# Recurrence gates of a hybrid attention and recurrence block: two passes per head over 64 rows in place of two over 128

## The chip, the cores and the metric

The kernel runs on one core of a Trainium2 chip. TensorE (PE) multiplies, VectorE (DVE), ScalarE (ACT) and GpSimd (POOL) do the rest, SyncE (SP), ScalarE and GpSimd issue transfers. The metric is the time of one execution on the device in microseconds.

## The reference

One layer: RMS norm, a combined projection, 16 heads of forgetting attention beside a recurrence over 1024 channels, an output projection, and a gated MLP with a convolution. All is float32, 512 tokens. The change is in the two gates of the recurrence:

```
def rg_lru(x, w_a, b_a, w_x, b_x, lam):
    xb = xf.reshape(B, S, N_RNN_BLOCKS, RNN_BLOCK)            # 16 blocks of 64 channels
    r = sigmoid(einsum('bsni,nij->bsnj', xb, w_a).reshape(B, S, D_RNN) + b_a)
    i_g = sigmoid(einsum('bsni,nij->bsnj', xb, w_x).reshape(B, S, D_RNN) + b_x)
    log_a = -RG_C * r * softplus(-lam)
    a = exp(log_a)
    mult = sqrt(-expm1(2.0 * log_a))
    bterm = mult * i_g * xf
    ...
```

So each block of 64 channels has a 64x64 matrix for each of two gates.

## The kernel before

Everything is computed transposed, with channels on the partitions and 512 tokens along the free axis. A float32 product is made of three TensorE passes: each operand is split into a rounded high part (ScalarE, `hi`) and the rest (VectorE, `lo`), and `product` adds high by high, high by low and low by high.

The mixer (the first 560 us) goes over 8 pairs of heads. A pair has 128 attention channels and 128 recurrence channels, and ten units of weights (512 KB each): two for each of x, q, k, v and the branch that goes through GeLU. SyncE loads a unit into `raw`, ScalarE's `split` writes the high part into `w_all`, VectorE's `split` the low part, and TensorE's `unit` waits for `split_done` and makes 48 passes of 256 columns. `w_all` holds two units, so ScalarE may write the next one only when `unit_used` says that TensorE is through with the one before last. Pair 0 is written out in the opening, pair 1 is `pair(1, True)`, and pairs 2 to 7 are a hardware loop over `pair(p, False)`. Each engine has its own `pair`, written by hand, and its own order.

For pair p, u is 10 p. TensorE makes units u and u+1 (x), transposes of the probabilities of the pair before, u+2 and u+3 (q), the attention values of the pair before, u+4 with the gates in its middle and u+5 (k), then u+6 with the scores in its middle and u+7 (v), transposes, u+8 and u+9. In pair 1 the gates stand in the middle of u+5.

The gates: `gw` holds for each gate a 128x128 matrix with the two 64x64 blocks of the pair on its diagonal and zeros beside them. It is loaded by GpSimd, split by ScalarE (`gate_weights`, `gw_hi`) and VectorE (`gw_lo`). TensorE's `gates` multiplies it with the convolved x (`xc_hi`, `xc_lo`), one bank for each gate. ScalarE's `gates` turns the banks into `rg` and `ig` by a sigmoid with a bias for each channel, lines 801 and 802. In the loop ScalarE's next piece of work behind them is the split of unit u+6; in pair 1 it is `k_hi`. GpSimd issues the load of `gw` for pair p, then that of `negc`, and then three rounds of sums of weights in memory, each of which waits for transfers. In the opening the load of `gw` is GpSimd's first instruction, and the memset of `ones` comes behind it; TensorE's `keep_busy` (18 float32 products of `ones`, before any work) waits for that memset.

The scores of a pair (line 2152) already run with 64 rows for each of two heads, the two heads' passes one after another into different banks.

Of the kernel before, what the change touches and what calls it, by code (L numbers as in the profile page):

```python
# [24 lines left out]
F32R = mybir.dt.float32r  # L25
ALU = mybir.AluOpType
ACT = mybir.ActivationFunctionType
AXX = mybir.AxisListType.X

P = 128  # L30
# [5 lines left out]
HD = 64  # L36
# [132 lines left out]
def block_kernel(nc, xT, par_d, weights, gate_w, out):  # L169
# [5 lines left out]
    with ExitStack() as ctx:  # L175
        def sb_in(stack, name, shape, dt=F32):
            return stack.enter_context(nc.sbuf_tensor(name, [P, *shape], dt))
# [38 lines left out]
        mix = ExitStack()  # L216
# [4 lines left out]
        xc_hi = sb_in(mix, "xc_hi", [S], F32R)  # L221
        xc_lo = sb_in(mix, "xc_lo", [S], F32R)
        gel = sb_in(mix, "gel", [S])
        rg = sb_in(mix, "rg", [S])
        ig = sb_in(mix, "ig", [S])
# [14 lines left out]
        sm = sb_in(mix, "sm", [CAUSAL])  # L240
        negc = sb_in(mix, "negc_sb", [2, S])
        pick = sb_in(mix, "pick", [2, P])
        gw = sb_in(mix, "gw", [2, P])
        gw_hi = sb_in(mix, "gw_hi", [2, P], F32R)
        gw_lo = sb_in(mix, "gw_lo", [2, P], F32R)
        stats = sb_in(mix, "stats", [3, QT])
        lam4 = sb_in(mix, "lam4", [NP])
        lam8 = sb_in(mix, "lam8", [NP])
# [9 lines left out]
        start = ExitStack()  # L258
# [102 lines left out]
        def col(name, i=0):  # L361

            c = COLS[name] + i
            return par[:, c:c + 1] if isinstance(c, int) else par[:, bass.ds(c, 1)]
# [222 lines left out]

        @block.gpsimd
        def _(pool):
            pool.dma_start(gw[:], gate_w[0]).then_inc(gw_landed, 16)  # L590
            pool.memset(eps[:], EPS)
            pool.memset(ones[:], 1.0).then_inc(consts_set, 1)
            pool.memset(ident[:], 0.0).then_inc(zeros_set, 1)
# [41 lines left out]
            sums(0, 2)  # L635
            for p in range(1, NP):
                pool.wait_ge(gw_split, p)
                pool.dma_start(gw[:], gate_w[p]).then_inc(gw_landed, 16)
                pool.wait_ge(s_taken, p * 6)
                pool.dma_start(negc[:], negc_d[2 * p:2 * p + 2].partition_broadcast(P)).then_inc(negc_landed, 16)  # L640
                sums(3 * p - 1, 3 * p + 2)
# [124 lines left out]
        def _(act):  # L766
# [30 lines left out]

            def gates(p, a, b):

                act.wait_ge(gates_done, p)  # L800
                act.activation(rg[:], a[:], ACT.Sigmoid, bias=col("b_a", p - 1)).then_inc(gates_taken, 1)
                act.activation(ig[:], b[:], ACT.Sigmoid, bias=col("b_x", p - 1)).then_inc(gates_taken, 1)

            def gate_exponentials(p):

                act.wait_ge(gates_taken, p * 2)
                act.activation(tt[:], rg[:], ACT.Tanh, scale=one_col(lam4, p - 1)).then_inc(gate_funcs, 1)
                act.activation(ae[:], rg[:], ACT.Exp, scale=one_col(lam8, p - 1)).then_inc(gate_funcs, 1)

# [6 lines left out]
                act.activation(gel[:], ev[:], ACT.Gelu_apprx_tanh).then_inc(gel_done, 1)  # L816

            def gate_weights(p):
                act.wait_ge(gw_landed, p * 16 + 16)
                act.activation(gw_hi[:], gw[:], ACT.Copy).then_inc(gw_hi_done, 1)  # L820

            def high_of(dst, src, taken, p, done):
# [340 lines left out]
            for i in range(NF):  # L1163
# [21 lines left out]
                if NS <= i < NS + 2 * PAIRS_OUT:  # L1185
                    n = i - NS
# [882 lines left out]
        def _(pe):  # L2069
            def product(dst, a, b, start, stop, goes_on=False):  # L2070

                (ah, al), (bh, bl) = a, b
                pe.matmul(dst, ah, bh, start=start, stop=False, skip_group_check=goes_on)  # L2073
                pe.matmul(dst, ah, bl, start=False, stop=False, skip_group_check=goes_on)  # L2074
                return pe.matmul(dst, al, bh, start=False, stop=stop, skip_group_check=goes_on)  # L2075
# [110 lines left out]
            def gates(p, a, b):  # L2186
                pe.wait_ge(gw_split, p + 1)
                pe.wait_ge(xc_split, p + 1)
                for g, bank in enumerate((a, b)):
                    last = product(bank[:], (gw_hi[:, g], gw_lo[:, g]), (xc_hi[:], xc_lo[:]), True, True)  # L2190
                last.then_inc(gates_done, 1)

            def pair_gates(p):
                pe.wait_ge(pt_split, p * 6)
# [2 lines left out]
            def pair_scores(p):  # L2197
                pe.wait_ge(q_split, p + 1)
                pe.wait_ge(k_split, p + 1)
                pe.wait_ge(gates_taken, p * 2 + 2)  # L2200
                scores((0, 1))

            def pair(p, first):
# [89 lines left out]
            gates(0, PT[0], PT[2])  # L2293
            unit(7, 1, 1, SB[2], False, True, middle=forget_back)
            pe.wait_ge(negc_ready, 1)
            pe.wait_ge(gates_taken, 2)
            for e, bank in enumerate((PT[0], PT[2])):
                last = pe.matmul(bank[:], pick[0:2 * NP, e], tt[0:2 * NP], start=True, stop=True)
            last.then_inc(negc_spread, 1)
# [30 lines left out]
            for c in range(3):  # L2330
                pe.wait_ge(split_done, N_OUT + c + 1)
                for j in range(4):
                    last = out_opening(c, j)
# [12 lines left out]
            for k in range(UK):  # L2346
                last = by_tokens(PJ[0], w_tile(0, k), k, k == 0, k == UK - 1)
            last.then_inc(unit_used, 1)
            pe.wait_ge(split_done, N_OUT + 6)
            for k in range(UK, KT):  # L2350
# [4 lines left out]
                last = by_tokens(PT[0], (w3_hi[:, i // 2, i % 2], w3_lo[:, i // 2, i % 2]), k, k == UK, k == KT - 1)  # L2355
# [17 lines left out]
            for n, bank in enumerate((OUT_BANKS[3][1], LAST_BANK)):  # L2373
                c = slice(HS * n, HS * n + HS)
                for i in range(UK):
                    last = product(bank[:, c], w_tile(1, i), (act_hi[:, UK + i, c], act_lo[:, UK + i, c]), i == 0,
                                   i == UK - 1)
# [6 lines left out]
            for j in range(QT):  # L2384
                if j == 0:
                    pe.wait_ge(osq_done, KT)
                if j == QT // 2:
                    pe.wait_ge(osq_done, KT + 1)
                last = pe.matmul(SB[2][:, j:j + 1], sq[:, 0, P * j:P * j + P], ones[:, 0:1], start=False, stop=j == QT - 1,
                                 skip_group_check=True)  # L2390
# [7 lines left out]
            for m in range(OPEN):  # L2398
                pe.wait_ge(split_done, N_FF + m + 1)
                for kt in range(2):  # L2400
                    k = 2 * m + kt
                    if k == 0:
# [4 lines left out]
                        for i, bank in enumerate((SB[0], SB[1], PT[0], PT[1])):  # L2407
                            last = half_by_tokens(bank, w_tile(0, 2 * i), 0, 1, True, False)
                        continue
                    pe.wait_ge(act_split, AFTER_Y + k + 1)  # L2410
                    for i, bank in enumerate((SB[0], SB[1], PT[0], PT[1])):
                        last = by_tokens(bank, w_tile(m % 2, 2 * i + kt), k, False, k == KT - 1)
# [160 lines left out]
```

## Time and profile before

| | us |
|---|---|
| median of 3 runs (lowest, highest) | 2149.89 (2149.03, 2150.46) |
| the profiled execution, its own time | 2149.89 |
| its span, first to last instruction | 2148.1 |
| TensorE busy in the span | 2116.0 |
| VectorE busy | 1685.9 |
| ScalarE busy | 1017.9 |
| GpSimd busy | 346.8 |

The granted clock of TensorE is 0.993 of full speed over the span. Times in the rows are counted from the span's start. A row of a timeline gives the start, the duration, the engine, the line and operation, output and inputs, the tile shape (rows by columns), the count where several are merged, and in brackets the idle time of that engine before it with what ended it. The duration of a TensorE pass includes its fill and drain, and passes overlap: what a pass costs is the distance to the next one's start, about 0.11 us for 256 columns and 0.23 us for 512.

### The profile page before, as it was taken

The page shows a single profiled execution, that of the slowest core. Times are in us where ns is not written, and L with a number is a line of the kernel's source. Part 1 is how long each engine was busy: PE and PEld are TensorE (multiplying, and loading weights), DVE is VectorE, ACT ScalarE, POOL GpSimd, SP SyncE. Part 2 cuts the span into 40 slices and gives each one's busy share as a digit, 9 for nine tenths or more (in the row PEclk, how much of TensorE's full clock was granted, in tenths as well). Part 3 has the DMA queues.
Part 4 walks back from the last instruction along what each step waited for, and adds up shares of the span by engine and source line. Part 5 has one row for each costly group of instructions (what it writes and reads, how often), then busy time and mean ns, then how long its engine had stood idle before and what let it go on. Part 6 is the DMA issues. An engine that isn't in the chain of part 4 may idle for free.

```text
span 2148.1 us, 44222 instructions
## 1 busy us (share of the span) xinstructions
PE 2116.0 (99%) x18226; PEld 2091.2 (97%) x18226; DVE 1685.9 (78%) x2298; ACT 1017.9 (47%) x1281; POOL 346.8 (16%) x431
## 2 busy tenths in 40 slices
PE   9999999999999999999999999999999999999995
PEld 8999999999999999999999999999999999999995
DVE  7777777778855877888888888888887767768886
ACT  6555554456322554444444444444444545445442
POOL 0222222222100001111111111211212001112003
PEclk9999999999999999999999999999999999999997
DMA  5788989888543436888878888787888658679544
GB/s 178 171 187 208 207 188 207 196 188 188 162 123 98 156 108 184 221 224 214 218 218 216 222 225 214 219 216 215 247 211 272 190 167 277 179 190 300 177 142 169
DMA packets 238755, 423.84 MB, mean 197 GB/s; under 512 B 17009, under 2 KB 151793, under 8 KB 237313
## 3 DMA queue, kind: packets, MB, share of 16 engines
q0 software_dynamic: 88224, 159.97, 35.9%
q1 hardware_dynamic: 147776, 256.84, 35.8%
q10 hardware_dynamic: 2592, 4.72, 0.6%
q8 instruction: 120, 1.97, 0.4%
q14 instruction: 43, 0.34, 0.1%
HBM read 382.64 MB, written 89.16 MB: 220 GB/s over the span
## 4 chain that ended last, share of the span: by engine, by line
PE 93%; DVE 3%; issue 1%; ACT 1%; POOL 1%; DMA 1%; POOLq 0%; DVEq 0%; ACTq 0%
PE bank L2073 29%; PE bank L2075 29%; PE bank L2074 29%; PE bank L2457 2%; PE bank L2152 1%; PE bank L2165 1%; DVE w_all L1219 1%; DMA act_lo_f<-t_spill 1%; PE bank L2177 0%; PE bank L2176 0%; ACT act_hi L1140 0%; ACT w_all L771 0%; PE bank L2237 0%; POOL act_lo_f L762 0%; POOL tsum_f L762 0%
## 5 line engine op out<-in xcount | busy, mean ns | idle before, releaser
L2073 PE MATMUL bank<-act_hi,w_all 128*128 128x256 f32 x3272 | 910.1, 278 | 4.8 <-DVE w_all L1219 2.2
L2074 PE MATMUL bank<-act_lo,w_all 128*128 128x256 f32 x3272 | 903.8, 276 | 0.0
L2075 PE MATMUL bank<-act_hi,w_all 128*128 128x256 f32 x3272 | 903.8, 276 | 0.0
L2073 PEld LDWEIGHTS bank<-act_hi,w_all 128*128 128x128 f32 x3272 | 614.3, 188 | 11.2 <-issue 3.7
L2074 PEld LDWEIGHTS bank<-act_lo,w_all 128*128 128x128 f32 x3272 | 614.4, 188 | 0.7 <-issue 0.2
L2075 PEld LDWEIGHTS bank<-act_hi,w_all 128*128 128x128 f32 x3272 | 614.4, 188 | 0.0
L2073 PE MATMUL bank<-tsum,w_all 128*128 128x256 f32 x1280 | 353.5, 276 | 0.0
L2075 PE MATMUL bank<-tsum,w_all 128*128 128x256 f32 x1280 | 353.3, 276 | 0.0
L2074 PE MATMUL bank<-tsum,w_all 128*128 128x256 f32 x1280 | 353.3, 276 | 0.0
L1134 ACT ACTIVATE w_all<-raw_s 128x1024 fp32r<-128x1024 f32 x172 | 182.7, 1062 | 243.3 <-PE bank L2075 222.7
L1219 DVE TENSOR_TENSOR w_all<-raw,w_all 128x1024 fp32r<-128x1024 f32 x134 | 164.0, 1224 | 133.6 <-ACT w_all L771 131.6
L1862 DVE TENSOR_TENSOR w_all<-raw_s,w_all 128x1024 fp32r<-128x1024 f32 x172 | 210.4, 1224 | 68.9 <-ACT w_all L1134 67.6
L2074 PEld LDWEIGHTS bank<-tsum,w_all 128*128 128x128 f32 x1280 | 240.2, 188 | 0.0
L2073 PEld LDWEIGHTS bank<-tsum,w_all 128*128 128x128 f32 x1280 | 240.2, 188 | 0.0
L2075 PEld LDWEIGHTS bank<-tsum,w_all 128*128 128x128 f32 x1280 | 240.2, 188 | 0.0
L771 ACT ACTIVATE w_all<-raw 128x1024 fp32r<-128x1024 f32 x133 | 140.6, 1057 | 162.4 <-PE bank L2075 157.5
L2073 PE MATMUL bank<-tsum,w 128*128 128x256 f32 x656 | 181.7, 277 | 0.2 <-DVE pu L1935 0.2
L2075 PE MATMUL bank<-tsum,w 128*128 128x256 f32 x656 | 181.2, 276 | 0.0
L2074 PE MATMUL bank<-tsum,w 128*128 128x256 f32 x656 | 181.2, 276 | 0.0
L2073 PE MATMUL bank<-act_hi,w 128*128 128x256 f32 x568 | 157.3, 277 | 0.0
L2075 PE MATMUL bank<-act_hi,w 128*128 128x256 f32 x568 | 156.8, 276 | 0.0
L2074 PE MATMUL bank<-act_lo,w 128*128 128x256 f32 x568 | 156.8, 276 | 0.0
(390 smaller groups left out, 3513.0 us busy)
## 6 DMA issues: line engine op xcount, KB each, us to landing
raw<-weights SPq DMA_DIRECT2D x262, 512.0 KB, 4.4
w_sums<-weights POOLq DMA_DIRECT2D x96, 512.0 KB, 7.0
raw_s<-weights SPq DMA_DIRECT2D x84, 512.0 KB, 5.7
raw_s<-weights POOLq DMA_DIRECT2D x84, 512.0 KB, 5.8
raw_a<-weights SPq DMA_DIRECT2D x66, 512.0 KB, 5.7
raw_s<-w_sums SPq DMA_DIRECT2D x48, 512.0 KB, 5.0
t_spill<-h_out POOLq DMA_DIRECT2D x48, 256.0 KB, 3.7
act_lo_f<-t_spill POOLq DMA_DIRECT2D x11, 1024.0 KB, 9.1
```

The costliest lines, as they stand in the source:

```text
L771: act.activation(w_hi[s], k_tiles(raw[:, s]), ACT.Copy).then_inc(hi_done, 1)
L1134: act.activation(w_slot(q)[0], k_tiles(RAW_OF[n](i)), ACT.Copy).then_inc(hi_done, 1)
L1219: dve.tensor_tensor(w_lo[s], k_tiles(raw[:, s]), word(w_hi[s]), ALU.subtract).then_inc(split_done, 1)
L1862: dve.tensor_tensor(lo, k_tiles(RAW_OF[n](i)), word(hi), ALU.subtract).then_inc(split_done, 1)
L2073: pe.matmul(dst, ah, bh, start=start, stop=False, skip_group_check=goes_on)
L2074: pe.matmul(dst, ah, bl, start=False, stop=False, skip_group_check=goes_on)
L2075: return pe.matmul(dst, al, bh, start=False, stop=stop, skip_group_check=goes_on)
L2152: last[e] = pe.matmul(dst, q, k, start=t == 0, stop=t == 2)
L2165: last = pe.transpose(dst, sm[:, c:c + P], ident[:])
L2457: last = pe.matmul(region, w[:, k // 2, k % 2], summed[:, k], start=start and k == 0, stop=k == UK - 1, skip_group_check=not start)
```

## The change

The two blocks of a gate no longer stand in one 128x128 matrix. For the even head `gw` holds on partitions 0 to 63 both gates' blocks side by side (64x128), for the odd head on partitions 64 to 127 the same with the gates exchanged. One pass over 64 rows gives both gates of one head. The products of the even head go to bank a (r gate on rows 0 to 63, i gate on rows 64 to 127), those of the odd head to bank b (i gate on rows 0 to 63, r gate on 64 to 127), the three parts of the product outermost, the two heads alternating. ScalarE now has four sigmoids of 64 rows, GpSimd three loads in place of one, and `gw`, `gw_hi` and `gw_lo` have 128 columns in place of 256.

```
-            pool.dma_start(gw[:], gate_w[0]).then_inc(gw_landed, 16)
+            def load_gates(p):
+                pool.dma_start(gw[0:HD], gate_w[p, 0:HD, :, 0:HD]).then_inc(gw_landed, 16)
+                for g in range(2):
+                    pool.dma_start(gw[HD:P, 1 - g], gate_w[p, HD:P, g, HD:P]).then_inc(gw_landed, 16)
+            load_gates(0)
...
-                act.wait_ge(gates_done, p)
-                act.activation(rg[:], a[:], ACT.Sigmoid, bias=col("b_a", p - 1)).then_inc(gates_taken, 1)
-                act.activation(ig[:], b[:], ACT.Sigmoid, bias=col("b_x", p - 1)).then_inc(gates_taken, 1)
+                act.wait_ge(gates_done, p * 2)
+                h0, h1 = slice(0, HD), slice(HD, P)
+                for dst, bias, parts in ((rg, "b_a", ((h0, a, h0), (h1, b, h1))), (ig, "b_x", ((h0, a, h1), (h1, b, h0)))):
+                    for h, bank, at in parts:
+                        act.activation(dst[h], bank[at], ACT.Sigmoid, bias=col(bias, p - 1)[h]).then_inc(gates_taken, 1)
...
-                for g, bank in enumerate((a, b)):
-                    last = product(bank[:], (gw_hi[:, g], gw_lo[:, g]), (xc_hi[:], xc_lo[:]), True, True)
-                last.then_inc(gates_done, 1)
+                for t, (w, x) in enumerate(((gw_hi, xc_hi), (gw_hi, xc_lo), (gw_lo, xc_hi))):
+                    for e, bank in enumerate((a, b)):
+                        h = slice(HD * e, HD * e + HD)
+                        last = pe.matmul(bank[:], w[h].rearrange("p a n -> p (a n)"), x[h], start=t == 0, stop=t == 2)
+                        if t == 2:
+                            last.then_inc(gates_done, 1)
```

The waits on `gw_landed`, `gates_done` and `gates_taken` have the new counts; nothing else moves. Line numbers of the changed kernel are a little higher.

TensorE in the loop, in the middle of unit u+4, before. Banks 5 and 6 are a and b, bank 3 takes k:

```order
L2075 MATMUL bank3<-act_hi,w_all 128x256
L2073 MATMUL bank5<-xc_hi,gw_hi 128x512 [waits xc_split,gw_split,pt_split]
L2074 MATMUL bank5<-xc_lo,gw_hi 128x512
L2075 MATMUL bank5<-xc_hi,gw_lo 128x512
L2073 MATMUL bank6<-xc_hi,gw_hi 128x512
L2074 MATMUL bank6<-xc_lo,gw_hi 128x512
L2075 MATMUL bank6<-xc_hi,gw_lo 128x512
L2073 MATMUL bank3<-act_hi,w_all 128x256
```

The same place in the changed kernel; each row of line 2201 is a pass over 64 rows (the shape is that of the output):

```order
L2084 MATMUL bank3<-act_hi,w_all 128x256
L2201 MATMUL bank5<-xc_hi,gw_hi 128x512 [waits xc_split,gw_split,pt_split]
L2201 MATMUL bank6<-xc_hi,gw_hi 128x512
L2201 MATMUL bank5<-xc_lo,gw_hi 128x512
L2201 MATMUL bank6<-xc_lo,gw_hi 128x512
L2201 MATMUL bank5<-xc_hi,gw_lo 128x512
L2201 MATMUL bank6<-xc_hi,gw_lo 128x512
L2082 MATMUL bank3<-act_hi,w_all 128x256
```

The number of passes is the same, the banks alternate. ScalarE in the loop, from the squares to the split of unit u+6 (the row of `w_all`), before:

```order
L842 ACTIVATE sq<-y_t 128x512
L801 ISA [waits gates_done]
L801 ACT_TABLE_LOAD
L801 ACTIVATE rg<-bank5,par 128x512
L802 ISA
L802 ACTIVATE ig<-bank6,par 128x512
L769 ISA
L145 REGISTER_ALU [waits raw_landed0]
L771 ACTIVATE w_all<-raw 128x4x2x128 [waits unit_used]
```

And in the changed kernel:

```order
L851 ACTIVATE sq<-y_t 128x512
L807 REGISTER_ALU
L811 ISA [waits gates_done]
L811 ACT_TABLE_LOAD
L811 ACTIVATE rg<-bank5,par 64x512
L811 ISA
L811 ACTIVATE rg<-bank6,par 64x512
L811 ISA
L811 ACTIVATE ig<-bank5,par 64x512
L811 ISA
L811 ACTIVATE ig<-bank6,par 64x512
L776 ISA
```

Two sigmoids and three register instructions more stand ahead of that split. GpSimd at the start of the program, before:

```order
L588 UNCONDITIONAL_BRANCH
L590 DMA gw<-gate_w 128x256
L591 MEMSET eps 128x1
L592 MEMSET ones 128x128
L593 MEMSET ident 128x128
```

And in the changed kernel:

```order
L589 UNCONDITIONAL_BRANCH
L593 DMA gw<-gate_w 64x2x64
L595 DMA gw<-gate_w 64x64 x2
L598 MEMSET eps 128x1
L599 MEMSET ones 128x128
```

The memset of `ones` has three issues ahead of it in place of one.

## Rows read from the trace of the kernel before

**Rows 1.** The page: busy time by engine, and the chain that ended last.
```profile
PE 2116.0 (99%) x18226; PEld 2091.2 (97%) x18226; DVE 1685.9 (78%) x2298; ACT 1017.9 (47%) x1281; POOL 346.8 (16%) x431
...
PE 93%; DVE 3%; issue 1%; ACT 1%; POOL 1%; DMA 1%; POOLq 0%; DVEq 0%; ACTq 0%
```

**Rows 2.** Timeline of TensorE, pair 7: first pass of the gates, first behind them.
```profile
491.23 0.39 PE L2073 MATMUL bank<-xc_hi,gw_hi 128*128 128x512 f32 x1
...
492.63 0.28 PE L2073 MATMUL bank<-act_hi,w_all 128*128 128x256 f32 x1
```

**Rows 3.** Timeline of TensorE, pair 7: into the scores and out of them.
```profile
503.48 0.28 PE L2075 MATMUL bank<-act_hi,w_all 128*128 128x256 f32 x1
503.68 0.50 PE L2152 MATMUL bank<-k_hi,q_hi 64*128 64x512 f32 x2
...
504.49 0.34 PE L2152 MATMUL bank<-k_hi,q_hi 64*128 64x384 f32 x2
...
505.60 0.28 PE L2152 MATMUL bank<-k_hi,q_lo 64*128 64x256 f32 x2
...
506.03 0.28 PE L2074 MATMUL bank<-act_lo,w_all 128*128 128x256 f32 x1
```

**Rows 4.** Timeline of ScalarE, pair 7: attention copies, sigmoids, split of unit 76.
```profile
492.45 1.08 ACT L834 ACTIVATE sm<-bank 64x512 f32<-64x512 f32 x2
...
497.19 0.69 ACT L801 ACTIVATE rg<-bank,par 128x512 f32<-128x512 f32 x1
497.78 0.68 ACT L802 ACTIVATE ig<-bank,par 128x512 f32<-128x512 f32 x1
498.35 1.06 ACT L771 ACTIVATE w_all<-raw 128x1024 fp32r<-128x1024 f32 x1
```

**Rows 5.** Timelines of VectorE and TensorE: unit u+6 in pairs 7 and 2.
```profile
499.44 1.23 DVE L1219 TENSOR_TENSOR w_all<-raw,w_all 128x1024 fp32r<-128x1024 f32 x1 [2.63 <-ACT w_all L771]
...
500.83 0.28 PE L2073 MATMUL bank<-act_hi,w_all 128*128 128x256 f32 x1
...
181.89 1.23 DVE L1219 TENSOR_TENSOR w_all<-raw,w_all 128x1024 fp32r<-128x1024 f32 x1 [2.63 <-ACT w_all L771]
...
183.17 0.38 PE L2073 MATMUL bank<-act_hi,w_all 128*128 128x256 f32 x1
183.39 0.28 PE L2074 MATMUL bank<-act_lo,w_all 128*128 128x256 f32 x1
```

**Rows 6.** Timelines of ScalarE and VectorE, pair 7: the split of unit 72.
```profile
468.69 1.06 ACT L771 ACTIVATE w_all<-raw 128x1024 fp32r<-128x1024 f32 x1 [0.46 <-PE bank L2075]
...
469.79 1.23 DVE L1219 TENSOR_TENSOR w_all<-raw,w_all 128x1024 fp32r<-128x1024 f32 x1 [2.20 <-ACT w_all L771]
```

**Rows 7.** Timelines of GpSimd, VectorE and TensorE: the start, and a small load.
```profile
1.27 0.68 POOL L590 DMA_DIRECT2D gw<-gate_w  x1 [0.81 <-POOLq L2565]
...
63.32 0.53 POOL L614 DMA_DIRECT2D negc<-tt  x1 [20.78 <-DVE tt L1300]
...
7.40 0.68 DVE L1507 TENSOR_TENSOR w_all<-raw,w_all 128x512 fp32r<-128x512 f32 x1
...
2.25 6.63 PE L2237 MATMUL bank<-ones 128*128 128x128 f32 x36 [2.25 <-POOL ones L592]
8.63 0.36 PE L2073 MATMUL bank<-act_hi,w_all 128*128 128x256 f32 x1
```

**Rows 8.** Timelines of ScalarE, VectorE and TensorE, pair 1: keys and scores.
```profile
120.65 0.63 ACT L824 ACTIVATE k_hi<-ev 128x512 fp32r<-128x512 f32 x1
...
121.31 0.69 DVE L1412 TENSOR_TENSOR k_lo<-ev,k_hi 128x512 fp32r<-128x512 f32 x1 [0.75 <-ACT k_hi L824]
...
122.43 0.50 PE L2152 MATMUL bank<-k_hi,q_hi 64*128 64x512 f32 x2
```

**Rows 9.** Timeline of ScalarE: k_hi in pair 0, split behind gw_hi in pair 1.
```profile
61.94 0.63 ACT L824 ACTIVATE k_hi<-ev 128x512 fp32r<-128x512 f32 x1 [1.51 <-DVE ev L1421]
...
106.30 1.06 ACT L771 ACTIVATE w_all<-raw 128x1024 fp32r<-128x1024 f32 x1 [1.80 <-DMA raw<-weights]
```

More of the change, by code:

```diff
@@ L242, in block_kernel @@
         pick = sb_in(mix, "pick", [2, P])
-        gw = sb_in(mix, "gw", [2, P])
-        gw_hi = sb_in(mix, "gw_hi", [2, P], F32R)
-        gw_lo = sb_in(mix, "gw_lo", [2, P], F32R)
+        gw = sb_in(mix, "gw", [2, HD])
+        gw_hi = sb_in(mix, "gw_hi", [2, HD], F32R)
+        gw_lo = sb_in(mix, "gw_lo", [2, HD], F32R)
+        sb_in(mix, "rest_of_gw", [6 * HD])
         stats = sb_in(mix, "stats", [3, QT])
@@ L637, in _ @@
                 pool.wait_ge(gw_split, p)
-                pool.dma_start(gw[:], gate_w[p]).then_inc(gw_landed, 16)
+                load_gates(p)
                 pool.wait_ge(s_taken, p * 6)
@@ L798, in gates @@
             def gates(p, a, b):
-                act.wait_ge(gates_done, p)
-                act.activation(rg[:], a[:], ACT.Sigmoid, bias=col("b_a", p - 1)).then_inc(gates_taken, 1)
-                act.activation(ig[:], b[:], ACT.Sigmoid, bias=col("b_x", p - 1)).then_inc(gates_taken, 1)
+                act.wait_ge(gates_done, p * 2)
[3 more added lines that the diff above has]
+                        act.activation(dst[h], bank[at], ACT.Sigmoid, bias=col(bias, p - 1)[h]).then_inc(gates_taken, 1)
             def gate_exponentials(p):
-                act.wait_ge(gates_taken, p * 2)
+                act.wait_ge(gates_taken, p * 4)
                 act.activation(tt[:], rg[:], ACT.Tanh, scale=one_col(lam4, p - 1)).then_inc(gate_funcs, 1)
@@ L818, in gate_weights @@
             def gate_weights(p):
-                act.wait_ge(gw_landed, p * 16 + 16)
+                act.wait_ge(gw_landed, p * 48 + 48)
                 act.activation(gw_hi[:], gw[:], ACT.Copy).then_inc(gw_hi_done, 1)
@@ L2199, in pair_scores @@
                 pe.wait_ge(k_split, p + 1)
-                pe.wait_ge(gates_taken, p * 2 + 2)
+                pe.wait_ge(gates_taken, p * 4 + 4)
                 scores((0, 1))
@@ L2295, in _ @@
             pe.wait_ge(negc_ready, 1)
-            pe.wait_ge(gates_taken, 2)
+            pe.wait_ge(gates_taken, 4)
             for e, bank in enumerate((PT[0], PT[2])):
```

## The prediction, made before the changed kernel was run

> **What bounds the kernel now.** First the page. TensorE is busy for 99% of the span and carries 93% of the chain that ended last [rows 1]. An edit pays only if it shortens TensorE's queue, and costs as soon as TensorE waits at a place where it does not wait now. ScalarE at 47% and VectorE at 78% look roomy, but those are averages. So I read next, around the gates, who releases TensorE's next weights and how long before it wants them. A unit here is one 512 KB block of weights, 48 passes of 256 columns.
>
> Take pair 7, the last turn of the loop. After the gates ScalarE converts the weights of unit 76 (the pair's u+6), VectorE subtracts, and TensorE may begin that unit. VectorE's subtraction starts at 499.44 and takes 1.23 us, so it ends at 500.67; TensorE starts the unit at 500.83 [rows 5]. The margin is 0.16 us. In pair 2 there is none: the subtraction ends at 183.12, TensorE starts at 183.17, and its next pass comes 0.22 us later where 0.11 is usual [rows 5]. Pair 4 reads as pair 2, pairs 3, 5 and 6 as pair 7. Six times the second path arrives in the very moment in which TensorE needs it.
>
> How is that path made? It starts from TensorE itself: ScalarE waits at 468.69 for the pair's first unit to be used up, and VectorE's subtraction follows at 469.79 [rows 6]. From there VectorE never idles for more than 0.2 us until 488.6, and from then on the two hand each other work (convolution, q, the two attention halves, the squares) with no wait for TensorE; ScalarE comes to its sigmoids at 497.19 straight from the squares and a table load [rows 4]. The gate products were ready at 492.6 plus the drain of the last pass, over 4 us earlier [rows 2]. So the sigmoids wait for ScalarE, not for TensorE, and everything added to them moves the end of the path.
>
> **TensorE's part of the change.** Six passes of 128 rows start at 491.23, and the next unit goes on at 492.63: 1.40 us [rows 2]. The new passes have the form of the scores: 64 rows, 512 columns, two side by side in two banks. There the last pass before starts at 503.48, so its successor would start at 503.59; three doubled steps of 512 columns are over at 504.49, which is 0.90 us with the entry [rows 3]. Leaving: the last doubled step starts at 505.60 with 256 columns, and the second pass after it at 506.03, where 505.60 + 0.12 + 0.11 = 505.83 would be natural, so 0.20 us [rows 3]. The new gates take 1.10 us, and TensorE is 0.30 us shorter each time. A doubled step alone costs half of two passes; the entry and the exit eat 0.4 of the 0.7 us.
>
> **ScalarE's part.** Two sigmoids of 128 rows become four of 64 rows. Starts are 0.59 and 0.57 us apart [rows 4]. Does half the rows halve it? The attention copies are 64x512, and two of them take 1.08 us [rows 4], so a narrow one is no cheaper than about 0.5 us. I take 2 x 0.585 = 1.17 us more; the lower bound is 4 x 0.49 - 1.17 = 0.8 (two copies, less the last one's tail), the upper 1.4 with about 0.05 us for each added register instruction, if they show.
>
> **Pairs 2 to 7.** The subtraction ends 1.17 us later: in pair 7 at 501.84, TensorE starts about 0.05 us after it as in pair 2, at 501.89, and pays the 0.11 us of a restart, against 500.83: +1.17. In pair 2, which restarts already, +1.17. TensorE arrives 0.30 us sooner, and only waits longer. The keys come next on ScalarE: k_lo ends about 1.2 us later too, and the scores then start half a unit (2.7 us) after the late start, so they don't wait a second time. After the scores TensorE makes one and a half units before it needs probabilities, and ScalarE and VectorE wait for it again; the delay isn't made up, for the next pair's path starts from TensorE. 6 x 1.17 = **+7.0 us**.
>
> **Pair 1** has another order: its unit 16 is converted before the gates, but the keys after. k_hi starts at 120.65 right behind the sigmoids, k_lo at 121.31 for 0.69 us, and the scores at 122.43 [rows 8]. 1.17 later, k_lo ends at 123.17 and the scores start at 123.2: +0.8, of which gw_lo, now half as wide and ahead of it on VectorE, gives back a little. **+0.7 us**. TensorE's 0.30 goes into that wait.
>
> **Pair 0** lies in the opening. ScalarE idles 1.51 us before k_hi [rows 9], which covers the 1.17. Should that cover go, k_hi would be late by what is missing, and the scores of the opening have several us in hand. TensorE keeps its gain: **-0.3 us**.
>
> **The loads.** One GpSimd load becomes three. At the start they stand ahead of the memset of ones that releases TensorE's warming passes. Those run from 2.25 until the first real pass at 8.63, although its weights were split at 7.40 + 0.68 = 8.08 [rows 7]. So the start hangs on GpSimd's queue. One issue takes 0.68 us there, a small one later 0.53 [rows 7]; two more cost 1.06 to 1.36, I take 1.2. The inputs have 0.55 us in hand already and now 1.7. TensorE has hardly a wait in the 70 us behind it, so nothing absorbs it: **+1.2 us**. In the loop the three loads, and the negc load and the sums queued behind them on GpSimd, come 1.1 to 1.4 us later. In pair 1 ScalarE waits for gw, but behind it 1.80 us more for raw [rows 9], which hides that; in later pairs gw_hi is followed by over 4 us of waiting for xc. If this cover were gone, pair 1 alone could lose 1 us. gw_hi and gw_lo are half as wide and lie in the same gaps in pairs 2 to 7: nothing.
>
> **Sum.** 7.0 + 0.7 + 1.2 - 0.3 = +8.6 us on the profiled execution, which took 2149.89 us (span 2148.1) and is itself the median of the three runs: **2158.5 us**, 0.40% slower. With the bounds: ScalarE at +0.8 gives 4.8 + 0.35 + 1.1 - 0.3 = +6.0; at +1.4 it gives 8.4 + 1.0 + 1.4 - 0.3 = +10.5. So 2155.5 to 2160.5.
>
> **Rivals.** (a) *The path has slack that I don't see*: VectorE makes up for the sigmoids, or the conversion of unit u+6 turns out not to end last. Then TensorE's 0.30 counts in all eight places and only the start costs: -2.4 + 1.2 = -1.2, 2148.7 us. For it: both engines have idle time on average. Against it: the rows of pair 2, where TensorE already waits.
>
> (b) *Faster*: as (a), and the doubled passes switch for nothing. One gate block then costs 3 x 0.23 = 0.70 in place of 1.40, eight save 5.6, less 1.2 at the start: -4.4, 2145.5 us. It decides as soon as ScalarE's 1.17 us is covered in the loop and the entry costs nothing. The scores, which show an entry and an exit of 0.2 us each [rows 3], speak against it.
>
> The Trainium skill, TensorE: Matmul & The Clock Gate, section Measured speedup vs the span model, has packed passes cost one pass and about 4 ns for each further tile, which is (b). TensorEngine Tiling (Array Packing), section Key Properties, says that changing the tiling mode drains the array; by that the block keeps the 1.10 us of my sum, and here the trace agrees: 0.4 us lie around each block of scores.
>
> (c) *Part of it*: half-row sigmoids run nearly in the time of the wide ones together, ScalarE adds 0.4 us or less. Pairs 2 to 7 then lose about 0.4 each, and the sum is 2.4 + 0 + 1.2 - 0.3 = +3.3, 2153.2 us. For it only that fewer rows are read; against it the copies [rows 4].
>
> (d) *The gate passes do not run side by side*, six one after another with the entry and the exit: 1.8 us where I take 1.1. In pairs 1 to 7 TensorE waits for the other path anyway, in pair 0 it costs 0.7 more: 2159.2.
>
> **Chances.** Forecast with (d) 78%, (c) 8%, (a) 9%, (b) 5%. This kernel's measurement tells some 0.2% (4.3 us) from no change, so slower by more 79%, within it 16%, faster by more 5%. The range 2153 to 2161.5 takes in (c) and the bounds with some run to run spread, and leaves (a) and (b) out.
>
> **What would show it.** In the profile after: four sigmoid rows about 0.58 us apart, and VectorE's subtraction for unit u+6 starting near 3.8 us (now 2.63) after its last work; TensorE with a wait of about 1.2 us released by that subtraction in each of pairs 2 to 7, and of about 1 us before the scores of pair 1; gate blocks of 1.1 us; the first real pass near 9.8 us instead of 8.63; a loop turn of 64.7 us where it is 63.5. Sigmoids at 0.3 us, or no wait of TensorE for the subtraction, would make the prediction wrong; so would a start that stays at 8.6.

## The result, and the profile after

| | before | after |
|---|---|---|
| median of 6 runs each (lowest, highest), us | 2150.18 (2148.33, 2150.95) | 2162.56 (2160.90, 2164.03) |
| span of the profiled execution, us | 2148.1 | 2159.0 |
| ScalarE busy, us | 1017.9 | 1029.2 |

The change costs 12.4 us, a ratio of 1.0059 with an interval of 1.0047 to 1.0070. Slower as forecast, but 4 us more than forecast, and outside the range. The profiled execution of the changed kernel took 2160.90 us, the fastest of its six, so that its trace shows 11 of the 12.4 us. One execution of the kernel before, of 27 in a later series, took 5546 us and one of eleven of e9 5407, and neither is in a ratio.

The page of the changed kernel, busy time, chain and the first row of the costliest groups (the line, then count, busy us and mean ns, then the idle time before it and who ended most of it):

```profile
PE 2113.1 (98%) x18226; PEld 2085.9 (97%) x18226; DVE 1685.7 (78%) x2298; ACT 1029.2 (48%) x1297; POOL 355.8 (16%) x447
...
PE 83%; DVE 9%; ACT 4%; issue 3%; POOL 1%; DMA 1%; DVEq 0%; ACTq 0%; POOLq 0%; SPq 0%
...
L2082 PE MATMUL bank<-act_hi,w_all 128*128 128x256 f32 x3272 | 911.2, 278 | 15.8 <-DVE w_all L1228 12.2
```

The chain, which was TensorE's at 93% [rows 1], now runs through VectorE and ScalarE for 13%. Who makes TensorE wait between 80 and 570 us, the loop of pairs, stands in the waits (us in total, times, longest):

```profile
PE bank L2082 <- DVE w_all L1228: 10.2, 6, 1.7
PE bank L2161 <- DVE k_lo L1421: 1.8, 1, 1.8
PE bank L2174 <- DVE sm L1348: 0.8, 1, 0.8
```

Six waits for the weights of unit u+6, one in each of pairs 2 to 7, and one for the keys in pair 1: the places that the prediction named. Its sizes do not fit. The third, at 95 us, for the probabilities of pair 0, is in the kernel before too, and is its only one in this stretch:

```profile
PE bank L2165 <- DVE sm L1339: 0.6, 1, 0.6
```

Pair 7, TensorE around the gates, which answers [rows 2]:

```profile
501.20 0.28 PE L2084 MATMUL bank<-act_hi,w_all 128*128 128x256 f32 x1
501.41 0.50 PE L2201 MATMUL bank<-xc_hi,gw_hi 64*128 64x512 f32 x2
501.75 0.40 PE L2201 MATMUL bank<-xc_lo,gw_hi 64*128 64x512 f32 x2
501.98 0.40 PE L2201 MATMUL bank<-xc_hi,gw_lo 64*128 64x512 f32 x2
502.31 0.38 PE L2082 MATMUL bank<-act_hi,w_all 128*128 128x256 f32 x1
502.53 0.28 PE L2083 MATMUL bank<-act_lo,w_all 128*128 128x256 f32 x1
```

The pass after the gates would follow the last one at 501.31; the second pass behind them starts at 502.53 where 502.31 + 0.11 would be natural. From 501.31 to 502.42 is 1.11 us for what took 1.40. TensorE's part is as forecast. Then ScalarE in the same pair, which answers [rows 4]:

```profile
505.98 1.28 ACT L811 ACT_TABLE_LOAD   x1
507.27 1.40 ACT L811 ACTIVATE rg<-bank,par 64x512 f32<-64x512 f32 x2
508.69 1.39 ACT L811 ACTIVATE ig<-bank,par 64x512 f32<-64x512 f32 x2
510.11 1.06 ACT L778 ACTIVATE w_all<-raw 128x1024 fp32r<-128x1024 f32 x1
```

From the first sigmoid to the split of u+6 it is 510.11 - 507.27 = 2.84 us. Before it was 1.16: 1.68 more, where the prediction has 1.17. VectorE and TensorE follow, answering [rows 5]:

```profile
511.20 1.22 DVE L1228 TENSOR_TENSOR w_all<-raw,w_all 128x1024 fp32r<-128x1024 f32 x1 [4.31 <-ACT w_all L778]
```

```profile
512.48 0.39 PE L2082 MATMUL bank<-act_hi,w_all 128*128 128x256 f32 x1 [1.70 <-DVE w_all L1228]
```

VectorE idles 4.31 us where it idled 2.63: the whole 1.68. TensorE stands still for 1.70. Pair 2 reads 186.63 with 1.72, pair 6 447.31 with 1.70. From pair 6 to pair 7 the chain needs 512.48 - 447.31 = 65.17 us, where a turn took 63.5.

Where the 11 us come from can be read off one event that both traces have, the first pass of each pair's scores (before; after; how much later):

| pair | before | after | later | added |
|---|---|---|---|---|
| 0 | 68.80 | 69.00 | 0.20 | 0.20 (0.50 by the start, 0.30 gained by the gates) |
| 1 | 122.43 | 124.42 | 1.99 | 1.79 (0.21 by the longer wait at 95 us, 1.58 behind it) |
| 2 | 186.12 | 189.59 | 3.47 | 1.48 |
| 3 | 249.62 | 254.76 | 5.14 | 1.67 |
| 4 | 313.20 | 319.92 | 6.72 | 1.58 |
| 5 | 376.73 | 385.09 | 8.36 | 1.64 |
| 6 | 440.18 | 450.26 | 10.08 | 1.72 |
| 7 | 503.68 | 515.42 | 11.74 | 1.66 |

Behind the loop the difference shrinks to 10.9. From 710.3 to 713.7 us TensorE's granted clock in before is at 1.2 GHz, which this execution of after has not, and across that stretch the difference falls from 11.74 to 11.24; the rest goes later, in small steps.

### The profile page after: what moved, and what is told of

The parts are those of the page before. It is cut to its first block, busy times and chain, and to the rows that moved or that the text cites. A ratio compares the mean times of both kernels' runs of the same rounds, so it can differ in the third digit from the quotient of the medians.

```text
span 2159.0 us, 44272 instructions
## 1 busy us (share of the span) xinstructions
PE 2113.1 (98%) x18226; PEld 2085.9 (97%) x18226; DVE 1685.7 (78%) x2298; ACT 1029.2 (48%) x1297; POOL 355.8 (16%) x447
## 4 chain that ended last, share of the span: by engine, by line
PE 83%; DVE 9%; ACT 4%; issue 3%; POOL 1%; DMA 1%; DVEq 0%; ACTq 0%; POOLq 0%; SPq 0%
PE bank L2082 26%; PE bank L2084 26%; PE bank L2083 26%; PE bank L2469 2%; DVE w_all L1228 1%; ACT w_all L778 1%; PE bank L2161 1%; DVE xc L1414 1%; DVE pt_lo L1315 0%; ACT ig L811 0%; ACT L811 0%; PE bank L2174 0%; DVE w L1381 0%; DVE y_t L1396 0%; DMA raw<-weights 0%
```

## Experiments

Every ratio is to the kernel before, measured in alternation on the same chip.

**Is it ScalarE alone, and what makes a narrow sigmoid so long?** The sigmoids of the changed kernel stand 0.71 us apart, those of before 0.58, and a narrow one takes 0.685 us, a wide one 0.69. Three kernels ask for the reason. Two change only the order of the four:

```
# as changed: (out rows, in rows) = (0,0) (64,64) (0,64) (64,0)
+ e1_out_rows: (0,0) (0,64) (64,64) (64,0)
+ e2_in_rows:  (0,0) (64,0) (64,64) (0,64)
```

> The changed kernel with ScalarE's four sigmoids in another order: r even, i even, r odd, i odd, so that the first two and the last two write the same rows, while the rows read change from each to the next. In the changed kernel the four start 0.71 us apart, the whole duration of one; before, two sigmoids of 128 rows started 0.59 us apart. Theory A (ScalarE lets the next instruction in early only if it writes the same rows): two of the four distances fall to 0.59 us, the block from 2.84 to 2.6 us, 8 us x 0.24 in all, so about 1.7 us less than the changed kernel, 2160.9. Theory B (the rows read decide): all four stay 0.71 us, and the time stays at 2162.6. Theory C (a narrow sigmoid with a bias never overlaps, in whatever order): the same as B.

> The changed kernel with the four sigmoids in the order r even, i odd, r odd, i even: the first two and the last two read the same rows of their banks, while the rows written change from each to the next. Theory A (rows written decide): all four distances stay 0.71 us, 2162.6. Theory B (rows read decide): two of them fall to 0.59 us, 2160.9. Theory C (never): 2162.6.

The third takes the kernel before and cuts each of its two sigmoids into two halves; TensorE and the loads stay.

```
-act.activation(rg[:], a[:], ACT.Sigmoid, bias=col("b_a", p - 1)).then_inc(gates_taken, 1)
-act.activation(ig[:], b[:], ACT.Sigmoid, bias=col("b_x", p - 1)).then_inc(gates_taken, 1)
+for dst, bias, bank in ((rg, "b_a", a), (ig, "b_x", b)):
+    for h in (slice(0, HD), slice(HD, P)):
+        act.activation(dst[h], bank[h], ACT.Sigmoid, bias=col(bias, p - 1)[h]).then_inc(gates_taken, 1)
```

> The kernel before with only ScalarE's part of the change: each of its two sigmoids in two halves of 64 rows, with the loads and TensorE's passes of before. If the longer sigmoid block is what costs (1.68 us more on the path to unit u+6), pairs 2 to 7 lose 1.5 to 1.6 us each, pair 1 about 1.7, pair 0 little: 2150.2 + 11 = 2161 us, nearly the whole loss. If the loads or the 64-row passes were behind a good part of it, it stays under 2157.

Measured: e1 2163.48, 1.0068 [1.0051, 1.0084]; e2 2160.98, 1.0053 [1.0036, 1.0069]; e3 2160.85, 1.0053 [1.0036, 1.0070]. So ScalarE's part alone, with no new pass on TensorE, is some 11 of the 12 us. The waits of e3, as above:

```profile
PE bank L2074 <- DVE w_all L1220: 8.5, 6, 1.4
PE bank L2153 <- DVE k_lo L1413: 1.3, 1, 1.3
```

The six are 0.3 us shorter each than in the changed kernel, because TensorE arrives later by just that. In e1 and e2 no order brings two sigmoids closer than 0.70, so A and B fall. C is left, and beside it a rule by which a change of either side is enough, since each step in both kernels changes at least one; the probe below tells the two apart. That e2's time is the one that theory B gave is luck, as its two steps did not shrink. Only one step shrinks, in e2 the last one, to the split:

```profile
507.93 0.69 ACT L810 ACTIVATE rg<-bank,par 64x512 f32<-64x512 f32 x1
508.65 0.69 ACT L810 ACTIVATE ig<-bank,par 64x512 f32<-64x512 f32 x1
509.24 1.05 ACT L778 ACTIVATE w_all<-raw 128x1024 fp32r<-128x1024 f32 x1
```

0.59 us, where all others have 0.71. That sigmoid writes from row 0 on, like the split.

**The start.** The changed kernel, with the first loads of `gw` behind the memset of ones on GpSimd:

```
-            load_gates(0)
             pool.memset(eps[:], EPS)
             pool.memset(ones[:], 1.0).then_inc(consts_set, 1)
+            load_gates(0)
```

> The changed kernel with the first three gate loads behind the memset of ones in place of ahead of it. In the changed kernel the first real pass of TensorE starts at 9.13 us, before at 8.63. The warming passes now start below 2 us and the first real pass should start at 8.1 to 8.6 us: 0.5 to 1 us less than the changed kernel, 2161.8 us. If the start is held by something else it stays at 9.1 and 2162.6.

Measured: 2162.02, 1.0057 [1.0040, 1.0073]. The first real pass starts at 8.36, in the changed kernel at 9.13 (9.55 and 9.52 in e1 and e2), before at 8.63. The scores of pair 0 start 0.67 us sooner than in the changed kernel and those of pair 1, at 123.25, 1.17 us sooner, so the start is on the path. The times do not show it (1.0057 beside the 1.0059 of the changed kernel). At the end none of it is left in the profile, and in pair 3 one sees why (a window, TensorE busy and its passes, the granted clock, the DMA engines' share, GB/s):

```profile
248.00:252.00 4.00, 1.99 (x15) 0.92 1.44 178
252.00:256.00 4.00, 4.00 (x24) 0.65 0.81 190
```

24 passes in 4 us where some 35 are usual: 3.4 us at 1.2 GHz, right behind a wait of 2.01 us that ends at 250.97. It cost this execution some 1.7 us. The other waits in the pairs, of 1.3 to 1.8 us, in this run and the others, had no such thing behind them.

**TensorE's part alone.** The changed kernel with its loads and its passes, and two sigmoids of 128 rows on the two banks. It leaves out sorting the halves of the banks into the two gates, so that only the r gate of the even head is right and the output is wrong; the work is the same:

```
-for dst, bias, parts in ((rg, "b_a", ((h0, a, h0), (h1, b, h1))), (ig, "b_x", ((h0, a, h1), (h1, b, h0)))):
-    for h, bank, at in parts:
-        act.activation(dst[h], bank[at], ACT.Sigmoid, bias=col(bias, p - 1)[h]).then_inc(gates_taken, 1)
+act.activation(rg[:], a[:], ACT.Sigmoid, bias=col("b_a", p - 1)).then_inc(gates_taken, 1)
+act.activation(ig[:], b[:], ACT.Sigmoid, bias=col("b_x", p - 1)).then_inc(gates_taken, 1)
```

> The changed kernel with its loads and 64-row passes, but ScalarE's two sigmoids of 128 rows as before. The banks hold r and i of a head one above the other, so each sigmoid mixes the gates and takes the wrong bias for half of its rows: the gates of the output are wrong, the work is that of the kernel before. Theory A (ScalarE's block is the whole loss in the loop; TensorE's 0.30 us in a pair can't be had there, since unit u+6 waits for ScalarE and VectorE anyway): pairs 2 to 7 turn in 63.5 us as before, pair 0 gains 0.3 and the start loses 0.5 to 1.2: 2150.2 + 0.5 = 2150.7 us. Theory B (TensorE's gain counts in the loop): 6 x 0.3 less, 2149.0, and a turn of 63.2 us.

Measured over 10 runs: 2149.53, 1.0002 [0.9993, 1.0012], as theory A has it. In pair 7 the unit before ends with a pass at 500.21, so that the next could start at 500.32; it starts at 500.54, restart included. From pair 6's scores to pair 7's it is 63.51 us, before 63.50. From pair 3 on TensorE's 0.30 us goes into waiting for unit u+6 and is worth nothing: the path through ScalarE sets the turn in the kernel before as well. In pair 1, where the keys' path has 0.4 us in hand, it does arrive: the scores start at 122.02, before at 122.43, and pair 2 gives half of that back (185.90, before 186.12).

**Which instructions of ScalarE overlap.** The kernel before, with groups of six instructions of 512 columns at its end, that compute nothing:

```
+for n, (o, i) in enumerate(pairs):      # o: rows written, i: rows read
+    act.activation(w_all[o, S * n:S * n + S], banks[2 + n % 2][i], func, **bias)
```

> The kernel before with eight groups of six ScalarE instructions added at its end, reading banks that are no longer used and writing places of the weights that are no longer used; 512 columns each. Copies: 1 all rows; 2 rows 0 to 63; 3 rows 0 to 63 and 64 to 127 by turns; 4 the same written, but rows 0 to 63 read each time; 5 rows 0 to 63 written, the two halves read by turns; 6 all rows and rows 0 to 63 by turns. Sigmoids with a bias: 7 rows 0 to 63; 8 the two halves by turns. Theory A (a change of the first row read or written keeps an instruction from starting before the one before it has ended; the number of rows does not matter): groups 1, 2, 6 and 7 step by 0.49 to 0.59 us, groups 3, 4, 5 and 8 by 0.65 to 0.72. Theory B (only a narrow sigmoid with a bias is slow): groups 1 to 6 step by 0.5, 7 and 8 by 0.7. Theory C (the number of rows matters): group 6 steps by 0.66 too.

| group | step, us | one takes, us |
|---|---|---|
| copies: all rows; rows 0-63; all rows and 0-63 by turns | 0.48 | 0.59 |
| copies, both sides by turns 0-63 and 64-127 | 0.605 | 0.59 |
| copies, only the rows written by turns | 0.605 | 0.59 |
| copies, only the rows read by turns | 0.605 | 0.59 |
| sigmoids, rows 0-63 | 0.575 | 0.68 |
| sigmoids, halves by turns | 0.70 | 0.68 |

Two neighbours of group 5 (only the rows read change), one of sigmoids on the same rows (two merged into one row), and one of sigmoids by turns:

```profile
2136.79 0.59 ACT L1218 ACTIVATE w_all<-bank 64x512 fp32r<-64x512 f32 x1
2137.39 0.59 ACT L1218 ACTIVATE w_all<-bank 64x512 fp32r<-64x512 f32 x1
...
2144.76 1.26 ACT L1218 ACTIVATE w_all<-bank,par 64x512 fp32r<-64x512 f32 x2
...
2148.34 0.68 ACT L1218 ACTIVATE w_all<-bank,par 64x512 fp32r<-64x512 f32 x1
2149.04 0.68 ACT L1218 ACTIVATE w_all<-bank,par 64x512 fp32r<-64x512 f32 x1
```

The number of rows doesn't matter, neither for one instruction nor for the overlap. What matters is where the rows begin: an instruction starts 0.10 to 0.12 us before its predecessor is through, unless its first row read or its first row written is another one.

This is theory A. That left the short step in e2, where the rows read begin at 64 and then at 0. A second probe of the same kind takes sources out of SBUF as well as PSUM, and has three groups on VectorE.

> The kernel before with six groups of six ScalarE copies (512 columns) and three groups of six VectorE copies at its end; they compute nothing. The first probe gave a step of 0.48 us from copy to copy where the first row that is read and written stays (128 or 64 rows, or by turns), and 0.605 where the first row read, the one written or both change, with 0.59 us for each copy by itself. Groups, ScalarE: 1 out of SBUF, all rows; 2 out of SBUF, halves by turns; 3 into rows 0 to 63, by turns from PSUM rows 64 to 127 and SBUF rows 0 to 63; 4 the same from rows 0 to 63 of both; 5 rows 0 to 31 and 32 to 63 by turns; 6 low half, high half, all rows. VectorE: 7 all rows, 8 rows 0 to 63, 9 halves by turns. Theory A (the overlap asks for the same first row on each side, whatever the memory): 2, 3, 5 at the duration of one, 1 and 4 some 0.11 us shorter; in 6 only the step from all rows to the low half is short. Theory B (each memory is looked at by itself, as the 0.59 us step from the last sigmoid, which reads rows 64 to 127 of PSUM, to the split, which reads all rows of SBUF, suggests): 3 is short as well. VectorE: if it has the same rule, 9 is longer than 8 by about 0.1 us each; if not, equal.

Measured steps: 1, out of SBUF, all rows, 0.52. 2, SBUF by turns, 0.64. 3, PSUM rows from 64 and SBUF rows from 0 by turns, 0.48 to 0.54, but the first step 0.61. 4, both from 0, 0.48 and 0.52. 5, rows 0-31 and 32-63 by turns, 0.60. 6, only the step from all rows to the low half is short, 0.49 against 0.60. The first four of group 3:

```profile
2130.43 0.59 ACT L1217 ACTIVATE w_all<-bank 64x512 fp32r<-64x512 f32 x1
2131.03 0.63 ACT L1217 ACTIVATE w_all<-raw 64x512 fp32r<-64x512 f32 x1
2131.57 0.58 ACT L1217 ACTIVATE w_all<-bank 64x512 fp32r<-64x512 f32 x1
2132.05 0.62 ACT L1217 ACTIVATE w_all<-raw 64x512 fp32r<-64x512 f32 x1
```

So theory B: each memory is compared with the last read from it. The long first step belongs to it, since the last read from SBUF before 2131.03 is that of group 2, which begins at row 64. VectorE, copies of all rows or of rows 0 to 63 one after another 0.60 us apart, halves by turns 0.70:

```profile
2144.59 1.28 DVE L2079 CAST w_all<-bank 128x512 fp32r<-128x512 f32 x2
...
2152.09 0.69 DVE L2079 CAST w_all<-bank 64x512 fp32r<-64x512 f32 x1
2152.80 0.68 DVE L2079 CAST w_all<-bank 64x512 fp32r<-64x512 f32 x1
```

The Trainium skill, VectorE: DVE Perf Modes, section Two Vector instructions with no wait between them, has this as a model for VectorE: an instruction is held until the earlier ones are finished if an input begins in another group of 32 rows than the last read from that memory, or the output in another than the last write to it. The VectorE groups agree, 0.70 against 0.60. That ScalarE behaves alike is what these runs add. The Trainium skill, ScalarE: Activation LUTs, section What ACT_TABLE_LOAD costs, says that consecutive ACTIVATEs overlap by some 93 ns; the probe has 0.10 to 0.12 us, and only where the first rows stay.

By this rule all steps of the four sigmoids are held, in any order: their (written, read) first rows are (0,0), (64,64), (0,64) and (64,0), and no two agree on both sides. Only the last step, to the split, can be saved, which is e2.

**Taking the sigmoids out of the way.** If the path through ScalarE sets the turn, the split of u+6 should go ahead of them: ScalarE has it waiting while the gates, ready for 4 us, are needed by nobody soon. The same edit in both kernels (the changed one also has the late loads of e4):

```
                 else:
-                    gates(p + 1, PT[0], PT[1])
                     split(u + 6, 0, MORE_MIX)
-                    gate_exponentials(p + 1)
+                    gates(p + 1, PT[0], PT[1])
                 high_of(k_hi, ev, k_taken, p, k_hi_done)
                 split(u + 7, 1, MORE_MIX)
-                if first:
-                    gate_exponentials(p + 1)
+                gate_exponentials(p + 1)
```

> The changed kernel with the first gate loads behind the memset of ones, and with ScalarE's order in pairs 2 to 7 changed: the split of unit u+6 ahead of the four sigmoids, the two exponentials behind the split of unit u+7. The sigmoids no longer stand ahead of that split, so the path to unit u+6 ends some 3 us before TensorE wants it, and k_hi follows the sigmoids, about when k is there. If ScalarE's block costs only by its place, TensorE doesn't wait in pairs 2 to 7, these lose nothing and gain TensorE's 0.3 each; pair 1 still loses 1.6, the start 0 to -0.3: 2150.2 - 2.1 + 1.6 - 0.2 = 2149.5 us, 13 less than the changed kernel. If the delay is only moved on (to the keys, the exponentials or the probabilities), 2155 or more.

> The kernel before with ScalarE's order in pairs 2 to 7 changed as in the run above (split of unit u+6 ahead of the two sigmoids, exponentials behind the split of unit u+7), nothing else. In pairs 2 and 4 TensorE waits 0.1 to 0.2 us for unit u+6, which should go: 2150.2 - 0.4 = 2149.8 us, no difference that can be measured. If the order were worth more by itself, the gain of the run above would be the order's and not the gates'.

Measured over 11 runs each: e7, the changed kernel, 2147.66, 0.9992 [0.9983, 1.0001]; e8, the kernel before, 2148.15, 0.9994 [0.9985, 1.0003]. Both are about 1 us less than expected beside the 2149.6 of before in this series, and neither is clear of no change. ScalarE of e7 in pair 7:

```profile
494.68 1.05 ACT L778 ACTIVATE w_all<-raw 128x1024 fp32r<-128x1024 f32 x1
495.76 1.28 ACT L811 ACT_TABLE_LOAD   x1
497.05 1.39 ACT L811 ACTIVATE rg<-bank,par 64x512 f32<-64x512 f32 x2
498.47 1.40 ACT L811 ACTIVATE ig<-bank,par 64x512 f32<-64x512 f32 x2
500.33 0.63 ACT L833 ACTIVATE k_hi<-ev 128x512 fp32r<-128x512 f32 x1 [0.47 <-DVE ev L1428]
```

The 2.84 us of sigmoids now fit ahead of the keys, here with 0.47 us left (2.33 in e8; in pair 3 nothing is left), and no pair waits for unit u+6 any more. From the scores of pair 6 to those of pair 7:

| kernel | from, to | us |
|---|---|---|
| before | 440.18, 503.68 | 63.50 |
| e5, passes alone | 439.97, 503.48 | 63.51 |
| e8, before reordered | 439.41, 502.87 | 63.46 |
| e7, changed and reordered | 439.06, 502.22 | 63.16 |

With the sigmoids off the path, and only then, TensorE's 0.30 us per pair arrives. One wait of this chain was left in e7, at pair 1, whose code is apart:

```profile
PE bank L2159 <- DVE k_lo L1419: 1.5, 1, 1.5
```

There ScalarE idles 2.83 us ahead of the squares. e9 is e7 with another order in that pair, gates and keys ahead of the squares, and on VectorE the keys ahead of adding the squares:

```
                 if first:
                     split(u + 6, 0, MORE_MIX)
+                    gates(p + 1, PT[0], PT[1])
+                    high_of(k_hi, ev, k_taken, p, k_hi_done)
                 attention_square(p)
                 recurrent_square(p)
```

> The reordered form of the changed kernel, and in the unrolled pair 1 alone ScalarE takes the four sigmoids and the high part of k ahead of the two squares, VectorE the scores' k ahead of adding the squares. In the reordered kernel's profile TensorE has one wait left in this chain: 1.46 us before the scores of pair 1 (at 123.26, for the low part of k). There ScalarE sat idle 2.83 us before the squares (to 116.49) while the gates' passes had ended at about 116.1. Theory A (each wait that goes moves the end by its length, as at TensorE's chain so far): sigmoids from 117.4, high part of k done by 120.9, low part by 121.6, scores at 121.7: 1.4 us less than the reordered kernel's 2147.66, some 2146.2, ratio 0.9985 to before. Theory B (the split of unit u+7, now behind the squares, becomes the wait that takes its place, or the start and the later stages vary by more): no wait for k_lo, but one for w_all at the next unit, 2147.5 and 0.999.

Measured over ten runs: 2146.26, 0.9985 [0.9976, 0.9994], theory A. The wait is gone and none takes its place; the scores of pair 1 start 1.3 us sooner than in e7, those of pair 7 2.4 us sooner than before:

```profile
501.24 0.50 PE L2161 MATMUL bank<-k_hi,q_hi 64*128 64x512 f32 x2
```

This is the lowest time of the study, and the only one whose interval lies below 1 (it overlaps that of e7): some 3 us under the kernel before, 16 under the change as made. Not all of it is the gates': the order alone has e8 some 1.3 us under before, itself not clear of no change. This last order was not tried in the kernel before, where TensorE has no wait for the keys in pair 1.

## Why the prediction was wrong in size

**Right.** *The bound*: margins of 0.16 us and none, the path that starts from TensorE anew each pair, so that each delay is paid in full and adds up. The table of scores shows it, and e3 shows it without the rest of the change. *TensorE's part*: 1.10 us for a block, read off the scores' entry and exit, and its gain swallowed in pairs 1 to 7 (by the waits of the changed kernel; in e5 from pair 3 on). *Pair 0*: -0.30, from +0.50 at the first pass to +0.20 at the scores. What the Trainium skill says in TensorEngine Tiling (Array Packing), Key Properties, agreed: with 0.2 us of entry and of exit, the block came to 1.10 and not 0.70. *Pair 1*: the keys wait, not unit 16. All four rivals fell: the waits answer (a), the entry and exit (b), sigmoids of 0.685 us (c), and (d) because the passes do run side by side.

**The step that failed** is ScalarE's price: "I take 2 x 0.585 = 1.17 us more; the lower bound is ... 0.8, the upper 1.4". It measured 1.68. The step took the distance between the two sigmoids of before, 0.59, as the price of any sigmoid. That distance holds 0.11 us of overlap, which two instructions with the same first rows have and the four new ones, by the probe, never have. Two more sigmoids are 2 x 0.575 = 1.15; four steps that lose their overlap are 4 x 0.12 = 0.5; together 1.65. In each of pairs 3 to 7 the turn then grows by 1.68, less the margin of 0.16, plus the 0.05 from the subtraction's end to TensorE and a restart of 0.11, as in the prediction's own sum: 1.68, measured 1.58 to 1.72. Six pairs gave 9.75 us instead of 7.0.

A hint stood in the trace of before, one line above the copies of [rows 4]:

```profile
491.79 0.63 ACT L824 ACTIVATE q_hi<-ev 128x512 fp32r<-128x512 f32 x1 [1.89 <-DVE ev L1416]
```

From this wide copy, 0.63 us long, to the first narrow one at 492.45 it is 0.66; between the narrow ones 0.49. By the rule of the memories that is a copy that waited for its predecessor to end, as the last read of PSUM before it began at row 0 and it begins at row 64; this one place was not tried by itself. The upper bound asked whether register instructions show. e1 to e3 don't need them: in the loop and in the probe, where no register is set, the steps of the sigmoids are alike, 0.71 and 0.70.

**Pair 1** cost 1.58 instead of 0.7. The form of the sum was right, the price less the 0.4 us that the keys had in hand; with 1.68 in place of 1.17 it gives 1.25. The rest is ahead of the sigmoids: the squares of pair 1, which wait for VectorE's `y_t`, start at 117.66 and not 117.03, 0.63 us late where TensorE was 0.41 late. This came from the weights of unit 15, beside [rows 9]:

```profile
107.24 1.06 ACT L778 ACTIVATE w_all<-raw 128x1024 fp32r<-128x1024 f32 x1 [1.86 <-DMA raw<-weights]
...
108.41 1.23 DVE L1228 TENSOR_TENSOR w_all<-raw,w_all 128x1024 fp32r<-128x1024 f32 x1 [0.39 <-ACT w_all L778]
```

The load landed 0.94 us later than before (106.30), and VectorE, which did not idle there before, waits 0.39 us for it. Whether the three loads of `gw` delay that one is not shown: e4 and e5 have them too, and there ScalarE starts on unit 15 6.3 and 6.6 us after it started on unit 14, here 7.3, before 6.7. From pair 0's scores to pair 1's e1, e2 and e4 need 1.3 to 1.4 us more than before, this execution 1.8.

**The start** was put at 1.2 and reads 0.50 in this execution, 0.9 in e1 and e2 and 0.16 in e5, all with the same loads, and -0.3 in e4. The price of the loads was right, what follows them was taken as rigid. Beside [rows 7]:

```profile
3.37 6.01 PE L2249 MATMUL bank<-ones 128*128 128x128 f32 x36 [3.37 <-POOL ones L599]
9.13 0.36 PE L2082 MATMUL bank<-act_hi,w_all 128*128 128x256 f32 x1
```

The warming passes begin 1.12 us later, but take 6.01 us in place of 6.63. They stand 0.21 us apart at first and 0.11 later, a factor of two as between 1.2 and 2.4 GHz. The switch came at 7.3 us in the trace of before, after 23 slow steps, and at 7.1 in this one, after 17; in e1 and e2 after 21 and 20, in e5, at 6.3 us, after 13. The fewer slow passes, the less is left of the 1.12 us.

Pair 0's 0.30 came in full, as the table shows, but then 0.21 is lost at 95 us, in the wait for the probabilities, 0.8 in place of 0.6 us. VectorE's four scalings of the probabilities (line 1339 before) begin 0.23 us later than before and end 0.42 later; why is open. The sum has +0.9 for start and pair 0, the trace 0.50 - 0.30 + 0.21 = +0.41. So the whole: 0.41 + 1.58 + 9.75 = 11.7 at the last scores, against 8.6.

**What stays open.** The profiled executions of before, e1, e2, e4, e5, e8, e9 and both probes have 3.4 us at 1.2 GHz that begin between 706 and 723 us, those of the changed kernel, e3 and e7 do not; why is not known. Single executions of one kernel differ by 3 us and more (before 2147.3 to 2150.8 in one series, e1 2161.2 to 2166.1), so that the 1.5 us between e1 and the change, each against its own runs of before, and the 0.5 between e7 and e8, are not read from times: the traces have 515.50 and 515.42 at pair 7's scores for e1 and the change, and 502.87 and 502.22 for e8 and e7.

## What to carry over

Before an edit is counted as a gain on the busiest engine, look at who releases it next: here 0.30 us on TensorE was bought with 1.68 us on an engine at 47%, and that engine's path was the one that ended last. Splitting an instruction of ScalarE or VectorE by rows makes neither half cheaper, and costs the overlap too whenever neighbours begin at different rows; price it by the duration of one, not by the distance of like neighbours. And a gain that is swallowed by a wait isn't lost: with work that nobody waits for moved behind the work that TensorE does wait for, the same passes gave their 0.30 us per pair.

## What the runs showed of the hardware

- ScalarE starts an instruction 0.10 to 0.12 us before the end of the last one if its first row read (from the same memory as the last read there) and its first row written are the same, otherwise not: copies 0.48 and 0.605 us apart, sigmoids 0.575 and 0.70. The number of rows (32, 64, 128) changes nothing.
- VectorE does likewise, copies out of PSUM 0.60 and 0.70 us apart.
- A stretch of 3.4 us at 1.2 GHz came once right behind a wait of TensorE of 2.0 us (e4, 250.97), and took with it more than the edit had gained. None came behind the waits of 1.3 to 1.8 us in the pairs.
- Four traces with the same first instructions (the change, e1, e2, e5) reach TensorE's fast passes, 0.11 us apart in place of 0.21, at 7.1, 8.0, 7.8 and 6.3 us, and with it the first real pass at 9.13, 9.55, 9.52 and 8.79.
